# Head 0's mask adds spread over the attention units, with a new order of the attention and delta stages, in an fp32 hybrid encoder layer

## The chip, the cores and the metric

The program runs on one core of a Trainium2 chip as one launch. The metric is device time in microseconds (us). TensorE (PE) does matmuls, VectorE (DVE) and ScalarE (ACT) elementwise work, GpSimd (POOL) elementwise work in SBUF, and SyncE's queue (SP) issues all transfers. Each engine takes its instructions in the order written and waits on semaphores.

## The reference

One encoder layer on 1536 tokens (a prompt of 1024, a sample of 512), width 1024. The two stages that matter here are neighbourhood attention and the gated delta rule.

```python
def row_block(args):                      # attention: 8 heads of 64, windows of 8 x 16 positions
    s = jnp.einsum("bjqhd,bijkhd->bhjqik", q_r, k_r).astype(jnp.float32)
    s = jnp.where(col_ok[:, :, None, :], s + bias, -jnp.inf)
    p = jax.nn.softmax(s.reshape(s.shape[:4] + (kh * NA_KB,)), axis=-1).reshape(s.shape)
    return jnp.einsum("bhjqik,bijkhd->bjqhd", p.astype(v.dtype), v_r)
...
# delta rule: 4 heads of 128, both directions; g is the running sum of the log decay in a chunk
decay = jnp.exp(jnp.where(incl, g[..., :, None] - g[..., None, :], -jnp.inf))
a_mat = jnp.einsum("bhnid,bhnjd->bhnij", k_beta, k) * jnp.where(strict, decay, 0.0)
sol = lax.linalg.triangular_solve(eye + a_mat, rhs, left_side=True, lower=True, unit_diagonal=True)
qk = jnp.einsum("bhnid,bhnjd->bhnij", q, k) * decay
def step(s, xs):
    v_new = u_c - jnp.einsum("bhck,bhkv->bhcv", w_c, s)
    o = jnp.einsum("bhck,bhkv->bhcv", qd_c, s) + jnp.einsum("bhij,bhjv->bhiv", qk_c, v_new)
    s = s * jnp.exp(gl_c)[..., None] + jnp.einsum("bhck,bhcv->bhkv", kd_c, v_new)
```

Before them runs one large projection (`front`), after them the branch merge (`merge_project`) and the MLP (`mlp`). These three stay as they are.

## The kernel before

**Attention** (`attention`) works through 48 units: 4 pairs of heads, and in each pair 12 units (3 groups of rows by 4 blocks of columns). Unit `u` goes through the engines in a fixed pipeline: TensorE scores (line 1159), VectorE adds the bias table and takes the maximum (line 1216, signals `biased`), ScalarE exponentiates (1277), VectorE normalises (1230, `na_pn`), TensorE transposes (1201), ScalarE copies (1287), TensorE mixes with the values (1188), VectorE copies the result out (1254). In the first 8 units of a pair TensorE also transposes the values (1171) for VectorE to copy (1240). The bias tables lie in 4 buffers; a table is loaded (1089) when its buffer's last user has signalled `biased`. A unit whose table is missing stops VectorE. All loads stand in one written order on the sync queue.

Delta head 0 is prepared during attention. The rows of its log decay come by a broadcast load into `dn_gq` (line 1110, issued at unit 1). GpSimd adds two masks to 6 pieces of it, 12 instructions (`strict` and `incl`, line 1139), into `dn_kb`, as soon as the load has landed. At unit 6 VectorE makes the per-token columns of the decay (`decay_columns`, lines 999 to 1006, 8 chained instructions). From unit 8 ScalarE spreads 48 exponentials over the remaining units (1267).

**The delta stage** (`deltanet`) takes 4 heads in turn. A head has two parts. In the *solve* part, 18 positions `k` (three levels of 6 groups, in the order of `ORDER`) go through TensorE (1766), ScalarE (1651, 1654), TensorE (1782), VectorE (1968 or 1971), TensorE (1798) and ScalarE (1644): block inverses are joined to larger ones in `dn_un` and `dn_tn`. Tables give the position at which side work stands: `TURN_AT` where TensorE transposes keys and values (1731), `TOKEN_AT` where VectorE scales those (1939), `COLUMNS_AT` where VectorE makes the next head's columns, `EG_AT` where ScalarE exponentiates the decay rows (1667), and the tables of the output norm of the head before (`SQUARES_AT` to `GATE_AT`). The transposes of `TURN_AT` share one PSUM bank, so each waits until the one before has been scaled twice.

In the *chain* part, 8 steps run the recurrence: TensorE 1817, VectorE 1994, TensorE 1821, ScalarE 1680, TensorE 1828 to 1836, then VectorE 2006 (the state) and ScalarE 1687 (the output). Beside it the next head is prepared: Gram matrices (1744), scores and queries times the decays (VectorE 1884, 1894), the cut of small blocks into `dn_c` (1905, 1625), a widening transpose (1913), the small inverses on GpSimd (1541 to 1549, a chain of 30), two transposes back (1919, 1920), and the placing of the blocks in `dn_un` (VectorE 1932) and `dn_tn` (ScalarE 1635, GpSimd 1559). The solve part of the next head begins after the placing.

## Time and profile before

| | |
|---|---|
| median of 3 runs | 3051.58 us (3047.43 to 3055.48) |
| the profiled execution, its own time | 3052.57 us |
| its span, first to last instruction | 3050.9 us |
| TensorE busy | 2883.6 us, 95% |
| VectorE, ScalarE, GpSimd busy | 1299.3, 1072.3, 1204.7 us |
| attention, first score to last pair's end | 1094.5 to about 1240 us of the span |
| delta stage | 1240.5 to 1638.0 us of the span |

A page of the profile gives busy times by engine; a timeline gives the instructions of one engine in order of start, like neighbours merged (`x4`), with the idle time ahead of them in brackets and what ended it. The granted clock is TensorE's, as a share of 2.4 GHz.

### The profile page before, as it was taken

The page shows a single profiled execution, that of the slowest core. Times are in us where ns is not written, and L with a number is a line of the kernel's source. Part 1 is how long each engine was busy: PE and PEld are TensorE (multiplying, and loading weights), DVE is VectorE, ACT ScalarE, POOL GpSimd, SP SyncE. Part 2 cuts the span into 40 slices and gives each one's busy share as a digit, 9 for nine tenths or more (in the row PEclk, how much of TensorE's full clock was granted, in tenths as well). Part 3 has the DMA queues.
Part 4 walks back from the last instruction along what each step waited for, and adds up shares of the span by engine and source line. Part 5 has one row for each costly group of instructions (what it writes and reads, how often), then busy time and mean ns, then how long its engine had stood idle before and what let it go on. Part 6 is the DMA issues. An engine that isn't in the chain of part 4 may idle for free. (4 is left out here: it accounts for less than half of the span.)

```text
span 3050.9 us, 38569 instructions
## 1 busy us (share of the span) xinstructions
PE 2883.6 (95%) x15219; PEld 2351.4 (77%) x15219; DVE 1299.3 (43%) x1953; ACT 1072.3 (35%) x1829; POOL 1204.7 (39%) x805
## 2 busy tenths in 40 slices
PE   6999999999999969588778999999999999999998
PEld 5878787877888846477667887878888888888887
DVE  5233233221479959666664352322233232232323
ACT  4241313243044539455543122332332323233232
POOL 2222122121123320433422423466666676756663
PEclk9999999999999979778899999999999999999999
DMA  4434233343545357210113545332323333333331
GB/s 115 169 131 139 80 102 102 100 128 98 177 155 168 129 190 250 79 53 22 74 47 119 172 155 201 99 111 86 108 85 95 97 97 124 99 95 96 114 108 56
DMA packets 239572, 352.78 MB, mean 116 GB/s; under 512 B 32929, under 2 KB 186273, under 8 KB 239393
## 3 DMA queue, kind: packets, MB, share of 16 engines
q1 hardware_dynamic: 239392, 350.32, 35.3%
q8 instruction: 122, 2.00, 0.3%
q14 instruction: 58, 0.47, 0.0%
HBM read 263.71 MB, written 96.36 MB: 118 GB/s over the span
## 5 line engine op out<-in xcount | busy, mean ns | idle before, releaser
L102 PE MATMUL pj_acc<-u_hi,pj_w_hi 128*128 128x512 f32 x1464 | 576.4, 394 | 10.6 <-DVE u_lo L823 10.6
L2774 DVE TENSOR_TENSOR x_tm<-m_ps,x_tm 128x512 f32<-128x512 f32 x384 | 265.0, 691 | 744.2 <-PE m_ps L104 744.2
L104 PE MATMUL pj_acc<-u_hi,pj_w_lo 128*128 128x512 f32 x1464 | 571.8, 391 | 0.0
L103 PE MATMUL pj_acc<-u_lo,pj_w_hi 128*128 128x512 f32 x1464 | 571.2, 390 | 0.0
L551 POOL TENSOR_TENSOR pj_w_lo<-pj_w_raw,pj_w_hi 128x1024 fp32r<-128x1024 f32 x61 | 159.3, 2612 | 721.6 <-ACT pj_w_hi L600 721.6
L2656 POOL TENSOR_TENSOR m_lo<-gate,held 128x1024 fp32r<-128x1024 f32 x96 | 237.9, 2501 | 269.8 <-ACT held L2573 269.8
L102 PEld LDWEIGHTS pj_acc<-u_hi,pj_w_hi 128*128 128x128 f32 x1464 | 275.8, 188 | 85.6 <-issue 18.2
L104 PEld LDWEIGHTS pj_acc<-u_hi,pj_w_lo 128*128 128x128 f32 x1464 | 275.8, 188 | 58.2
L103 PEld LDWEIGHTS pj_acc<-u_lo,pj_w_hi 128*128 128x128 f32 x1464 | 276.1, 189 | 56.2
L102 PE MATMUL m_ps<-held 128*128 128x512 f32 x768 | 298.9, 389 | 2.4 <-DVEq L2755 2.4
L102 PE MATMUL m_ps<-held,m_h_hi 128*128 128x512 f32 x768 | 299.5, 390 | 0.0
L104 PE MATMUL m_ps<-held,m_h_lo 128*128 128x512 f32 x768 | 298.8, 389 | 0.0
L103 PE MATMUL m_ps<-m_lo,m_h_hi 128*128 128x512 f32 x768 | 298.8, 389 | 0.0
L104 PE MATMUL m_ps<-held,m_lo 128*128 128x512 f32 x768 | 298.8, 389 | 0.0
L103 PE MATMUL m_ps<-m_lo,held 128*128 128x512 f32 x768 | 298.8, 389 | 0.0
L2649 POOL TENSOR_TENSOR m_lo<-gate,held 128x1024 fp32r<-128x1024 f32 x92 | 218.5, 2396 | 0.0
L600 ACT CAST pj_w_hi<-pj_w_raw 128x1024 fp32r<-128x1024 f32 x61 | 63.9, 1047 | 374.6 <-PE pj_acc L104 374.6
L2573 ACT CAST held<-gate 128x1024 fp32r<-128x1024 f32 x96 | 96.1, 1050 | 253.7 <-PE m_ps L104 247.6
L2585 ACT CAST m_h_hi<-m_rel 128x512 fp32r<-128x512 f32 x96 | 59.6, 621 | 356.1 <-POOL m_rel L2662 356.1
L2317 POOL TENSOR_TENSOR mo_w_lo<-mo_w_raw,mo_w_hi 128x512 fp32r<-128x512 f32 x71 | 96.8, 1364 | 197.6 <-ACT mo_w_hi L2255 197.6
L102 PEld LDWEIGHTS m_ps<-held 128*128 128x128 f32 x768 | 144.1, 188 | 32.6 <-DVEq L2755 2.8
L103 PEld LDWEIGHTS m_ps<-m_lo,held 128*128 128x128 f32 x768 | 144.1, 188 | 30.1
(308 smaller groups left out, 4930.9 us busy)
## 6 DMA issues: line engine op xcount, KB each, us to landing
gate<-in_w_mlp_dram SPq DMA_DIRECT2D x48, 1024.0 KB, 5.4
gate<-in_w_mlp_dram SPq DMA_DIRECT2D x96, 512.0 KB, 3.7
proj<-pj_stage SPq DMA_DIRECT2D x61, 768.0 KB, 3.4
pj_w_raw<-in_w_in_dram SPq DMA_DIRECT2D x61, 512.0 KB, 5.2
gate<-proj SPq DMA_DIRECT2D x24, 768.0 KB, 4.4
mo_w_raw<-in_w_out_dram SPq DMA_DIRECT2D x48, 256.0 KB, 2.9
rpb_bias<-pj_shut SPq DMA_DIRECT2D x48, 192.0 KB, 3.0
rpb_bias<-rpb_near SPq DMA_DIRECT2D x24, 384.0 KB
```

Of the source, the lines that this page charges most:

```text
L102: pe.matmul(out, w_hi, x_hi, start=first, stop=False)
L103: pe.matmul(out, w_hi, x_lo, start=False, stop=False)
L104: return pe.matmul(out, w_lo, x_hi, start=False, stop=last)
L551: pool.tensor_tensor(w_lo[:, n % 2], w_raw[:, n % 2], w_hi[:, n % 2].bitcast(F32), ALU.subtract).then_inc(lo_done, 1)
L600: act.copy(w_hi[:, n % 2], w_raw[:, n % 2]).then_inc(hi_done, 1)
L2317: pool.tensor_tensor(w_lo[:, sl % 2], raw_w(sl), w_hi[:, sl % 2].bitcast(F32), ALU.subtract).then_inc(w_lo_done, 1)
L2573: act.copy(views.w2_hi(2 * gg + j), w2_raw[:, j].rearrange("p (a n) -> p a n", a=2)).then_inc(w2_hi_done, 1)
L2585: act.copy(h_hi[:, m % 4], rel[:, j]).then_inc(hh_done, 1)
L2649: pool.tensor_tensor(views.w1_lo(m), w1_raw[:, :, j * P:(j + 1) * P], views.w1_hi(m).bitcast(F32), ALU.subtract).then_inc(w1_lo_done, 1)
L2656: pool.tensor_tensor(views.w2_lo(m), w2_raw[:, j].rearrange("p (a n) -> p a n", a=2), views.w2_hi(m).bitcast(F32), ALU.subtract).then_inc( ...
L2774: dve.tensor_tensor(xt, ps2[:, q % 4], xt, ALU.add).then_inc(added, 1)
```

## The change

The log-decay columns are no longer copied for each head. Two tiles for all heads, `gneg` (minus g) and `gbeta` (g plus ln beta), are made at the start of attention by three VectorE instructions and one ScalarE logarithm; `cx`, also for all heads, is made once at the start of the delta stage, with two small matmuls that pick the chunk ends out. As ln beta is in the exponent, the scores are multiplied by one 128x512 instruction in place of four 128x128. In attention the loads of pair 1 move to units 4 and 6, the decay rows to unit 8, the exponentials to unit 14, and each mask add waits for a unit: the first for unit 9, each further one for two units more. In the delta stage the tables are new, the placing is split anew between VectorE and ScalarE, GpSimd's product with the queries (1531) is cut in three for each direction and starts after the placing, and the row exponentials move from the solve part to steps 5 and 6 of the chain before.

```diff
@@ attention
-    DG_AT, DCOL_AT, DY_AT, DEXP_AT = 1, 6, (28, 32, 36), 8
+    MASK_AT = 10
+    DG_AT, PAIR1_AT, DCOL_AT, DY_AT, DEXP_AT = 8, (4, 6), 6, (28, 32, 36), 14
...
-            for a in range(2):
-                load_qk(1, a)
-                load_v(1, a)
...
+                if u in PAIR1_AT:
+                    load_qk(1, PAIR1_AT.index(u))
+                    load_v(1, PAIR1_AT.index(u))
...
                 for q, mask in enumerate((strict, incl)):
+                    pool.wait_ge(biased, 2 * (MASK_AT + 2 * (2 * n + q)))
                     pool.tensor_tensor(dd0[:, 2 * n + q], gq[:, 0, d, tg * TB:(tg + 1) * TB].rearrange("p (j n) -> p j n", n=P),
...
+            dve.tensor_scalar(gbeta[:], cols[:, :, 2:4], 1e-30, None, ALU.max).then_inc(d_rates, 1)
+            dve.tensor_scalar(gneg[:], cols[:, :, 0:2], -1.0, None, ALU.mult).then_inc(d_cols, 1)
...
                 if u == DCOL_AT:
-                    dve.wait_ge(dg_in, 32)
-                    dc = Chain(dve, d_chain, 0, 8)
-                    decay_columns(dve, dc, cols[:, 0], col2[:, 0], ncol2[:, 0], cx2[:, 0], gq[:, 0])
-                    dve.sem_inc(d_cols, 1)
-                    dc.end()
+                    dve.wait_ge(d_rates, 2)
+                    dve.tensor_tensor(gbeta[:], cols[:, :, 0:2], gbeta[:], ALU.add).then_inc(d_cols, 1)
...
+            rates = gbeta[:].rearrange("p h d t -> p (h d t)")
+            act.wait_ge(d_rates, 1)
+            act.activation(rates, rates, ACT.Ln).then_inc(d_rates, 1)
@@ deltanet
-SQUARES_AT, ROOT_AT, EG_AT, CEXP_AT = 1, 5, (0, 2), 10
-LENGTHS_AT, MEAN_AT, DIAG_AT, SPREAD_AT, NORM_AT, GATE_AT = 2, 3, 5, (7, 9, 11), (8, 10, 12), 12
-TURN_AT = (0, 3, 6, 9, 11, 13)
-TOKEN_AT = ((1, 2), (4, 5), (7, 8), (10, 11), (12, 13), (14, 15))
-COLUMNS_AT = 6
-INCL_AT = {8: 4, 11: 5, 13: 0, 15: 1}
+SUM_AT, SQUARES_AT, LENGTHS_AT, MEAN_AT, ROOT_AT, DIAG_AT = 0, 2, (3, 4, 5), 6, 8, 8
+SPREAD_AT, NORM_AT, GATE_AT = (10, 12, 14), (11, 13, 15), 15
+TURN_AT = (0, 2, 5, 8, 11, 13)
+TOKEN_AT = ((0, 1), (2, 3), (5, 6), (9, 10), (11, 12), (13, 14))
+INCL_AT = {9: 4, 12: 5, 15: 0}
...
-INCL_END = {1: 3, 3: 2}
+INCL_END = {1: 1, 3: 3, 4: 2}
...
-QK_IN = {0: (4, 5), 1: (0, 1), 4: (3, 2)}
+QK_IN = {0: (4, 5), 2: (0, 1), 5: (3, 2)}
...
+EG_IN = (5, 6)
...
+                for q in Q32:
+                    act.copy(by_direction(un, q, 0)[:, 0:NTB:2, :, q], compact(c1, q, 0)[:, 0:NTB:2]).then_inc(S["un0_d0"], 1)
+                act.wait_ge(S["spread"], 2 * i + 2)
                 for q in Q32:
                     act.copy(by_direction(tn, q, 0)[:, :, :, q], compact(c2, q, 0)).then_inc(S["tn0_act"], 1)
...
-                for j in range(4):
-                    last = dve.scalar_tensor_tensor(am[:, n, j], ps[:, 4 + 2 * (GRAMS.index(tg) % 2), j],
-                                                    ncol2[:, i % 2, 2 + d, 4 * tg + j:4 * tg + j + 1], decays[:, j], ALU.mult, ALU.mult)
-                last.then_inc(S["am_done"], 1)
+                dve.scalar_tensor_tensor(am[:, n], ps[:, 4 + 2 * (GRAMS.index(tg) % 2)], -1.0, decays, ALU.mult,
+                                         ALU.mult).then_inc(S["am_done"], 1)
...
-                if i:
-                    out_sum(i - 1)
...
+                        if k == SUM_AT:
+                            out_sum(i - 1)
```

The sync engine's queue in the first attention pair, before: the rows behind the first bias tables (`na_bias`) are pair 1's queries, keys and values, then the decay rows.

```order
L1089 DMA na_bias<-rpb_bias 128x2x384
L1075 DMA na_qt<-proj 128x512
L1075 DMA na_kt<-proj 128x768
L1080 DMA na_vt<-proj 128x2x384
L1080 DMA na_vt<-v_mid 128x2x384
L1075 DMA na_qt<-proj 128x1024
L1075 DMA na_kt<-proj 128x768
L1080 DMA na_vt<-proj 128x2x384
L1080 DMA na_vt<-v_mid 128x2x384
L1110 DMA dn_gq<-g_rows 128x1536 x2
L1089 DMA na_bias<-rpb_bias 128x2x384 x2
L1089 DMA na_bias<-rpb_bias 128x2x256 x3
```

The same place of the queue after the change.

```order
L1077 DMA na_bias<-rpb_bias 128x2x384 x3
L1077 DMA na_bias<-rpb_bias 128x2x256
L1063 DMA na_qt<-proj 128x512
L1063 DMA na_kt<-proj 128x768
L1068 DMA na_vt<-proj 128x2x384
L1068 DMA na_vt<-v_mid 128x2x384
L1077 DMA na_bias<-rpb_bias 128x2x256
L1063 DMA na_qt<-proj 128x1024
L1063 DMA na_kt<-proj 128x768
L1068 DMA na_vt<-proj 128x2x384
L1068 DMA na_vt<-v_mid 128x2x384
L1077 DMA na_bias<-rpb_bias 128x2x256
```

Four bias loads now stand ahead of the first of pair 1's loads, and one more between the two halves; before, one did, and the next came behind the decay rows.

VectorE in the solve part of delta head 0, from the last two positions of level 0, before.

```order
L1968 COPY_PREDICATED dn_un<-join,dn_ps 128x512
L1939 TENSOR_TENSOR dn_kb<-dn_ps,dn_col 128x512
L1971 COPY dn_un<-dn_ps 32x4x32 x2
L999 COPY dn_col<-cols 128x48
L1000 TENSOR_SCALAR dn_ncol<-dn_col 128x48
L1004 COPY dn_cx<-dn_col 128x12
L1005 TENSOR_TENSOR dn_cx<-dn_gq,dn_col 128x12
L1006 COPY dn_cx<-dn_gq 128x12
L1004 COPY dn_cx<-dn_col 128x12
L1005 TENSOR_TENSOR dn_cx<-dn_gq,dn_col 128x12
L1006 COPY dn_cx<-dn_gq 128x12
L1971 COPY dn_un<-dn_ps 32x4x32 x2
```

The same place after the change.

```order
L1971 COPY_PREDICATED dn_un<-join,dn_ps 128x512
L1950 TENSOR_TENSOR dn_kb<-dn_ps,cols 128x512
L1971 COPY_PREDICATED dn_un<-join,dn_ps 128x512 x2
L1950 TENSOR_TENSOR dn_kb<-dn_ps,dn_cx 128x512
L1974 COPY dn_un<-dn_ps 32x4x32 x2
L1950 TENSOR_TENSOR dn_kb<-dn_ps,dn_cx 128x512
L1974 COPY dn_un<-dn_ps 32x4x32 x6
L1950 TENSOR_TENSOR dn_kb<-dn_ps,cols 128x512
```

The eight column instructions between two positions of level 1 are gone, and the scalings `dn_kb` stand closer behind the positions.

ScalarE in steps 2 to 7 of the chain beside which the next head is prepared, after the change (`dn_nb` and `oz` are the recurrence's own copies).

```order
L1668 COPY dn_nb<-dn_ps 128x128 x4
L1617 COPY dn_c<-dn_am 32x384 x4
L1677 COPY oz<-dn_ps 128x128 x4
L1668 COPY dn_nb<-dn_ps 128x128 x4
L1677 COPY oz<-dn_ps 128x128 x4
L1591 ACTIVATE dn_qk<-dn_qk,dn_gneg 128x128 x4
L1668 COPY dn_nb<-dn_ps 128x128 x2
L1677 COPY oz<-dn_ps 128x128 x2
L1591 ACTIVATE dn_qk<-dn_qk,dn_gneg 128x128 x4
...
L1606 ACTIVATE dn_gq<-dn_gq 128x1536
L1668 COPY dn_nb<-dn_ps 128x128 x2
L1677 COPY oz<-dn_ps 128x128 x2
L1606 ACTIVATE dn_gq<-dn_gq 128x1536
```

The cut (`dn_c`) stands ahead of step 2's output copies where it stood behind them, and the two row exponentials (`dn_gq`) stand in steps 5 and 6, where there were none.

## Rows read from the trace of the kernel before

**Rows 1.** The page of the whole execution: its span, and the granted clock in 40 slices.

```profile
span 3050.9 us, 38569 instructions
...
PEclk9999999999999979778899999999999999999999
```

**Rows 2.** Windows: length, busy us of PE, PEld, DVE, ACT, POOL, clock, DMA.

```profile
1094.50:1145.00 50.50, 35.27 (x232) 22.11 (x232) 33.19 (x100) 21.66 (x66) 16.36 (x17) 0.75 0.63 223
1145.00:1174.90 29.90, 29.90 (x266) 19.74 (x266) 27.05 (x105) 26.97 (x88) 0.00 (x0) 1.00 0.75 238
...
1240.50:1276.10 35.60, 7.49 (x48) 7.14 (x48) 20.18 (x44) 3.54 (x7) 19.50 (x38) 0.63 0.36 141
1276.10:1321.65 45.55, 38.77 (x569) 33.80 (x569) 24.43 (x57) 25.96 (x69) 21.81 (x14) 0.69 0.01 2
1321.65:1359.40 37.75, 32.80 (x250) 29.68 (x248) 28.38 (x77) 20.01 (x72) 11.75 (x30) 1.00 0.00 1
...
1364.50:1419.50 55.00, 44.91 (x598) 37.02 (x599) 29.44 (x65) 29.82 (x72) 23.23 (x14) 0.75 0.20 76
...
1462.90:1515.20 52.30, 42.68 (x599) 35.86 (x600) 29.31 (x65) 29.70 (x72) 23.22 (x14) 0.79 0.21 79
...
1558.20:1603.70 45.50, 37.64 (x583) 30.88 (x583) 27.96 (x56) 20.21 (x43) 8.28 (x2) 0.84 0.20 69
```

**Rows 3.** Timeline, VectorE, first attention pair: start, us, instruction, idle before.

```profile
1119.56 0.56 DVE L1216 CUSTOM_DVE_ANT_0 na_sc<-na_ps_s,na_bias 128x384 f32<-128x384 f32 x1 [7.91 <-DMA na_bias<-rpb_bias]
...
1120.71 1.78 DVE L1230 TENSOR_SCALAR na_pn<-na_pr,na_rinv 128x384 f32<-128x384 f32 x2
...
1124.22 2.19 DVE L1230 TENSOR_SCALAR na_pn<-na_pr,na_rinv 128x384 f32<-128x384 f32 x2
...
1127.72 1.09 DVE L999 COPY dn_col<-cols 128x48 f32<-128x48 f32 x1
...
1133.76 0.16 DVE L1006 COPY dn_cx<-dn_gq 128x12 f32<-128x12 f32 x1
...
1135.51 0.75 DVE L1230 TENSOR_SCALAR na_pn<-na_pr,na_rinv 128x384 f32<-128x384 f32 x2
```

**Rows 4.** Timeline, the sync engine's queue, first attention pair.

```profile
1104.40 1.45 SPq L1110 DMA_DIRECT2D dn_gq<-g_rows  x2
1105.90 18.60 SPq L1089 DMA_DIRECT2D na_bias<-rpb_bias  x5
```

**Rows 5.** Timeline, GpSimd, first and last of head 0's twelve mask adds.

```profile
1118.45 1.26 POOL L1139 TENSOR_TENSOR dn_kb<-dn_gq,strict 128x512 f32<-128x512 f32 x1 [22.52 <-DMA dn_gq<-g_rows]
...
1132.39 1.26 POOL L1139 TENSOR_TENSOR dn_kb<-dn_gq,incl 128x512 f32<-128x512 f32 x1
```

**Rows 6.** Timeline, VectorE, one normalising multiply beside a mask add.

```profile
1121.08 1.42 DVE L1230 TENSOR_SCALAR na_pn<-na_pr,na_rinv 128x384 f32<-128x384 f32 x1
```

**Rows 7.** Waits of TensorE in the delta stage: total us, times, longest.

```profile
PE dn_ps L1766 <- DVE dn_un L1932: 40.8, 4, 25.6
PE dn_ps L1731 <- DVE dn_kb L1939: 21.6, 13, 3.9
```

**Rows 8.** Timeline, VectorE, delta stage, heads 0 and 1.

```profile
1290.37 0.99 DVE L999 COPY dn_col<-cols 128x48 f32<-128x48 f32 x1
...
1294.44 0.59 DVE L1971 COPY dn_un<-dn_ps 32x128 f32<-32x128 f32 x2 [0.26 <-DVE dn_cx L1006]
...
1334.75 2.15 DVE L1884 SCALAR_TENSOR_TENSOR dn_am<-dn_ps,dn_ncol,dn_am 128x128 f32<-128x128 f32 x8
...
1362.74 4.86 DVE L1932 COPY dn_un<-dn_c 32x256 f32<-32x256 f32 x16
```

**Rows 9.** Timeline, ScalarE, delta stage, head 0's row exponential.

```profile
1277.90 1.48 ACT L1667 ACTIVATE dn_gq<-dn_gq 128x1536 f32<-128x1536 f32 x1
```

**Rows 10.** Timeline, VectorE, the output gate of two heads.

```profile
1406.54 2.30 DVE L1869 SCALAR_TENSOR_TENSOR oz<-oz 128x1536 f32<-128x1536 f32 x1
...
1594.11 1.76 DVE L1869 SCALAR_TENSOR_TENSOR oz<-oz 128x1536 f32<-128x1536 f32 x1
```

More of the change, by code:

```diff
@@ L1682, in main @@
                         strict_decays(i + 1, STRICT_MID[step])
+                    if more and step == CUT_IN:
+                        cut_blocks(i + 1)
                     for j, d, t in live_chains(step):
@@ L1701, in _ @@
             act.wait_ge(mixed_landed, 16)
-            act.sem_inc(S["cexp"], 1)
             act.sem_inc(S["exp_s"], NG6)
             act.sem_inc(S["exp_i"], NG6)
+            act.wait_ge(S["columns"], 5)
+            flat_cx = cx[:].rearrange("p h a t -> p (h a t)")
+            act.activation(flat_cx, flat_cx, ACT.Exp).then_inc(S["cexp"], 1)
+            for d in range(2):
+                row_decays(0, d)
             cut_blocks(0)
@@ L1836, in main @@
                         pe.matmul(o, nb[:, j], qk2[:, i % 2, 2 * (t // 4) + d, t % 4], start=step == 0, stop=True).then_inc(S["o_mm"], 1)
+            pe.wait_ge(S["ends"], 2)
+            for d in range(2):
+                last = pe.matmul(ps[:, 3, d, 0:HEADS * NT], work[:, d * P:(d + 1) * P], cols[:, :, d], start=True, stop=True)
+            last.then_inc(S["ends"], 1)
             for x in range(NTB):
@@ L1984, in main @@
                             out_gate(i - 1)
-                    if k == COLUMNS_AT and more:
-                        columns(i + 1, nxt)
                 dve.sem_inc(S["s0"], 1)
@@ L2039 @@
                 K_KEPT.append((_step, _j))
-K_DN = 1 + 7 + 1
 class MlpViews:
```

173 lines of the change are left out of this document (84 added, 89 removed).

## The prediction

> **What bounds the kernel now.** I read the page first. The span is 3050.9 us, and the clock row has its dip in the slices of the delta stage [rows 1]. TensorE is busy 95% of the span, so only time in which it waits, or runs at a lower clock, can be won. The windows say where: the first attention pair's disturbed stretch takes 50.50 us at a granted clock of 0.75, and the next equal piece of work 29.90 at 1.00, PE busy throughout. The stretch in which delta head 0 is prepared takes 35.6 us with PE busy for 7.49. The four solve parts take 45.55, 55.00, 52.30 and 45.50 us at clocks of 0.69 to 0.84, head 0's chain part 37.75 us with 32.80 of PE [rows 2].
>
> Then the waits. In the attention stretch VectorE stands still for 7.91 us at 1119.56 for a bias table, and 8 column instructions fill it from 1127.72 to 1133.92 [rows 3]. In the delta stage TensorE waits 40.8 us in 4 waits for the placing of blocks (the longest, 25.6, is head 0's) and 21.6 us in 13 waits for the scalings of keys and values [rows 7].
>
> **The change part by part.** The sum is made against the profiled execution, 3052.57 us, 1.0 above the median.
>
> *Attention, loads.* The first bias table that VectorE waits for stands behind pair 1's loads and the decay rows; the five bias issues occupy the queue from 1105.90 for 18.60 us [rows 4]. Now four tables stand ahead of pair 1. The wait of 7.91 should go: −7.9. What is late next: pair 1's own queries and keys, wanted only about 20 us after the last of them is issued, and the decay rows, issued after unit 8 for a first mask at unit 9 and exponentials at unit 14. At 29.9/12 = 2.5 us a unit the last have some 12 us to land; if late, ScalarE, which works in order, would hold the probabilities back. I count nothing.
>
> *Attention, columns.* Seven of the eight chained instructions go from VectorE, 1127.72 to 1133.92 [rows 3]; −6.2. One addition of 128x96 stays; its nearest rows are 0.16 us (128x12) and 1.09 (128x48, beside GpSimd), and I take +0.5 for it and the three at the start. ScalarE's logarithm and the return to its exponential stand before the first score's exponential, where nothing is ready: 0.
>
> *Attention, masks.* Before, the twelve adds run from 1118.45 to 1133.65 [rows 5], partly inside the bias wait. Normalising multiplies beside them take 1.78 and 2.19 us the pair, 0.75 later without them [rows 3]: 1.78 + 2.19 − 1.50 = 2.5 us. In one go that is −2.5 when they leave. The whole gain of loads, columns and contention is 7.9 + 6.2 − 0.5 + 2.5 = 16.1, and with an estimated 1 for the clock of 0.75 in that stretch 17; its bounds are 14 (the wait and the columns alone) and 20.6 (50.50 − 29.90 [rows 2]).
>
> Spread, each add is released by `biased` of the last head of a unit, just as VectorE ends that addition and turns to the normalising multiply. So the add of 1.26 us falls on a multiply nearly every time, and a single multiply beside an add takes 1.42 in place of 0.75/2 = 0.38 [rows 6]: 1.04 us, twelve times 12.5. VectorE is busy 27.05 of 29.90 us in a steady stretch, 0.24 us a unit to spare, and TensorE has no idle time at all in it [rows 2]. The delay can therefore be hidden only in part, in the buffers between engines. Bounds: 0 (all in buffers) and 12 × 2 × 1.04 = 25 (both multiplies of a unit hit). I take 10, between 12.5 and that slack (12 × 0.24 = 2.9). Attention: −17 + 10 = −7.
>
> A rule speaks against this part too. The Trainium skill, "SBUF — State Buffer", section "SBUF: two separate sides", says that VectorE and GpSimd share a port pair, and that some of VectorE's fast or two-input instructions and a GpSimd instruction lock it against each other for the whole instruction. By that rule the multiply waits for the add's end, 1.26 + 0.38 = 1.64 at worst; the trace's 1.42 is close to it. By it the twelve would cost 15 in place of 12.5.
>
> *Head 0's preparation.* 35.6 us before [rows 2]. The 8 multiplies of 128x128 become 2, the row exponentials come before the cut, and two tiny matmuls for the chunk ends, with VectorE's copies for them, stand ahead of the Gram matrices. With the multiply's eight at 2.15 us [rows 8] as a gain of about 1, and one exponential of 1.48 [rows 9] plus about 1 for the ends as a loss: +1, bounds −2 to +4.
>
> *Placing.* VectorE's 16 copies take 4.86 us (0.30 each) [rows 8] and end what TensorE waits for. Less head 0's 25.6, the other three waits sum to 15.2, 5.1 a head [rows 7]. Now ScalarE places one part of `dn_un` after the first narrowing transpose while VectorE does the other after the second; the copies are about halved on each path. I take a third of the 4.86, 1.6 a head, four times −6; bounds 0 and −10 (half of it, 2.4, each).
>
> *Columns in the solve part.* Head 0's set for head 1 runs from 1290.37 until the next position's copy at 1294.44, 0.26 us of idle time among it [rows 8]; the position it holds back is on the path: about 3 of the 4.07 us, since some of it fits the loop's slack. In heads 1 and 2 no GpSimd work lies beside it and each is nearer 1: −5, bounds −2 and −10.
>
> *Turns and scalings.* The 21.6 us in 13 waits [rows 7] come where `TURN_AT` and `TOKEN_AT` leave a transpose waiting for a scaling of the position just before it, or the same. In the new tables turns and scalings stand one to three positions apart except at 11 and 13, where the columns are also gone. I take −13 of the 21.6, bounds −5 and −20.
>
> *Row exponentials.* In the solve part's opening ScalarE works on one of 1.48 us [rows 9] before positions' squares, −2 in all for a part of 1.48 in some heads. In the chain they now stand in steps 5 and 6, where ScalarE is busy 20.01 of 37.75 us [rows 2]: two of 1.48 are cheap unless an output copy or `dn_nb` waits behind one. The cut goes ahead of step 2's copies, am falls from 2.15 for 8 to perhaps 1.4 (its four reads are the same bytes, three starts are saved). Net +1 for the chain parts, bounds −3 and +9 (3 heads × 2 × 1.48).
>
> *Out_sum behind position 0 and the tables of the norm.* These are VectorE instructions that take the columns' place in the early positions. Where GpSimd works beside VectorE a large one lasts longer: 2.30 against 1.76 [rows 10]. A third-size piece has 0.2 to 1 us extra; it is in the bounds, not in the sum. The page just named, in the same section, would make such pieces wait for all of a GpSimd product; no row of before shows that pairing.
>
> *Clock.* Solve parts run at 0.69 to 0.84, that is partly at 1.2 GHz, and chains at 1.00 [rows 2]. Each low stretch follows a wait in which TensorE stood. Fewer waits, shorter low stretches: PE is busy 38.77 of 45.55 us at 0.69 in head 0. I take −5 for all; bounds 0 and −20, as head 3's part at 0.84 needs 37.64 of PE where heads 1 and 2 need 44.91 and 42.68 with head-norm work included.
>
> Sum: −7 + 1 − 6 − 5 − 13 − 2 + 1 − 5 = −36. 3052.57 − 36 = 3016.6 for a profiled execution, 3016 for the median.
>
> **The rivals.**
> *A, the clock stays up* (0.10). If the removed waits are those after which the clock falls, the solve parts would come near the PE time of full clock: for it speaks that the dips in [rows 1] lie only in this stage; against, that other waits (the solve loop's own, head 0's 25.6) remain. It would give 20 in place of 5 and some of the attention bounds: 2998 or less.
> *B, the small gain* (0.13). Each mask add hits both multiplies (25 in place of 10, net +8), and the row exponentials hold up steps 5 and 6 (+9 in place of +1). Then −36 + 15 + 8 = −13: 3039. For it: a pair of multiplies among back-to-back adds went from 0.75 to 2.19 [rows 3], 1.44 more and so more than one hit. Against: an add of 1.26 us is over when the multiply of 1.42 that it meets is, and the buffers between engines take some.
> *C, it doesn't do what it says* (0.08). The solve loop runs from engine to engine at its own latency; with the scaling waits gone, TensorE waits for the next position instead. Head 3's part, which has no next head's turns, still takes 45.50 [rows 2]. Then turns and columns give 4 in place of 18 (+14), the clock nothing (+5), placing half (+3), the opening nothing (+2) and head 0's preparation costs its upper bound (+3): −36 + 27 = −9, 3043, no change that can be told.
> *D, slower* (0.07). One mechanism: the chain parts fall to 1.2 GHz. Now they start from a solve part whose side work is elsewhere, and exponentials and cuts in ScalarE's order stop TensorE in steps 2, 5 and 6. A chain holds 32.80 us of PE at clock 1.00 [rows 2]; at 1.2 GHz that work is nearly twice as long, less the 5 us of idle time that it fills: 32.8 − 5 = about +28 each. One chain would give 3044, two 3072. The 36 us won are outweighed from 1.3 chains on, so it takes two. Against it: before, chains keep 1.00 in spite of the waits in them.
>
> **How the numbers follow.** Main forecast 3016, its own range 3000 to 3032, from the sum's bounds taken together, not all at their ends: 0.62. Between the cases: A 0.10 below 3000, B 0.13, C 0.08, D 0.07. The range 2994 to 3037 leaves out part of A, C, D and half of B. A measurement of this kernel tells about 0.3% from no change: 3042.4 to 3060.7. Main, A and B lie below it: 0.85; C lies within: 0.08; D is above: 0.07.
>
> **What would show each step right or wrong.** Attention: no wait of VectorE for a bias table above 1 us, no columns, and a first pair of about 33 us for the stretch that took 50.5; multiplies of 1.4 us beside the twelve adds, one a second unit. Delta: the placing waits after head 0's at 3.5 or less; the scalings' waits under 9 in all; solve parts of about 41, 48, 47 and 43; chain parts within 1 of before, clock 1.00. The prediction is wrong if masks cost nothing or twice as much in the pairs' lengths, if the waits for scalings come back under another name (for squares, or for `dn_un`), if the decay rows land late, or if the clock of the chains falls below 1.

## The result and the profile after

| | before | after |
|---|---|---|
| median | 3051.58 us | 3034.57 us |
| four runs | 3047.43 to 3055.48 | 3030.89 to 3036.73 |
| ratio | | 0.9942, 95% interval 0.9926 to 0.9958 |
| span of the profiled execution | 3050.9 us | 3031.9 us |

The change wins 17 us, 0.6%. The forecast was 3016 (-36), with a range of 2994 to 3037. The sign is right and the range holds the time, but the main case's own range, 3000 to 3032, does not, and the gain is less than half of what was worked out.

The page of the changed kernel, its span and granted clock [rows 1]:

```profile
span 3031.9 us, 38463 instructions
...
PEclk9999999999999999798879999999999999999999
```

The windows of the changed kernel, one for each stage: attention, head 0's preparation, then solve part and chain part of each head in turn (a chain part here reaches to the next solve part, so it holds the placing), and last all that follows. Columns as in [rows 2].

```profile
1093.70:1228.75 135.05, 124.79 (x1056) 80.28 (x1056) 118.75 (x416) 106.43 (x336) 16.39 (x18) 0.97 0.68 232
1228.75:1267.96 39.21, 9.32 (x54) 9.01 (x53) 19.82 (x30) 6.79 (x12) 19.06 (x38) 0.62 0.33 128
1267.96:1301.95 33.99, 32.15 (x568) 28.00 (x569) 21.09 (x48) 23.16 (x64) 22.96 (x19) 0.85 0.01 2
1301.95:1342.83 40.88, 33.64 (x250) 30.29 (x249) 29.17 (x61) 25.73 (x84) 13.33 (x34) 0.99 0.03 12
1342.83:1391.94 49.11, 41.05 (x599) 34.33 (x599) 29.45 (x56) 23.75 (x57) 24.35 (x19) 0.83 0.25 95
...
1433.47:1485.63 52.16, 43.67 (x598) 35.77 (x599) 29.48 (x56) 23.88 (x57) 24.35 (x19) 0.76 0.24 90
...
1527.02:1579.66 52.64, 44.88 (x582) 36.89 (x583) 29.71 (x56) 19.18 (x43) 9.38 (x7) 0.71 0.10 33
1579.66:1619.79 40.13, 31.51 (x217) 28.42 (x217) 15.74 (x43) 17.28 (x56) 1.27 (x1) 0.92 0.25 85
1619.79:3031.90 1412.11, 1396.96 (x6174) 1153.94 (x6174) 446.83 (x535) 414.71 (x568) 811.83 (x475) 0.99 0.35 113
```

The same stages of both kernels, lengths in us, cut at the same instructions in the windows of either trace:

| stage | before | after | difference |
|---|---|---|---|
| attention | 144.99 | 135.05 | -9.9 |
| head 0's preparation | 36.58 | 39.21 | +2.6 |
| solve part 0 | 45.51 | 33.99 | -11.5 |
| solve part 1 | 55.09 | 49.11 | -6.0 |
| solve part 2 | 52.24 | 52.16 | -0.1 |
| solve part 3 | 45.44 | 52.64 | +7.2 |
| chain parts 0 to 2 | 129.25 | 123.80 | -5.5 |
| chain part 3 | 38.60 | 40.13 | +1.5 |
| merge and MLP (same code) | 1408.63 | 1412.11 | +3.5 |

The reader is to see that TensorE's instructions are the same in both solve parts 3 (some 583 matmuls), yet its busy time rose from 37.64 [rows 2] to 44.88 us and the clock fell from 0.84 to 0.71; its idle time in that part stayed at 7.8 us. The gain shrinks from solve part to solve part, and the last one is slower than before. The merge and MLP differ by 3.5 us with the same code. In the other traces below this stretch is either 1408.6 to 1410.7 or 1411.8 to 1412.9, in kernels that differ only far ahead of it. TensorE is busy for 1396.96 us of the 1412.11 here, and for 1393.87 of 1409.03 with the same instructions in one of the kernels below, so the difference is in its clock. One profiled execution carries some 3 us of such chance, and what follows goes by medians and by single stages.

The waits of TensorE in the changed kernel, which answer to [rows 7]:

```profile
PE dn_ps L1762 <- ACT dn_un L1628: 31.0, 4, 23.4
...
PE dn_ps L1725 <- DVE dn_kb L1950: 7.1, 4, 2.9
...
PE dn_ps L1762 <- ACT dn_ss L1650: 5.4, 4, 2.5
PE dn_ps L1738 <- DVE dn_un L1974: 5.2, 3, 2.5
```

The waits for scalings fell from 21.6 to 7.1 us, as forecast. But what is left of them is one wait a head, 0.5, 1.4, 2.3 and 2.9 us, at position 2. The waits for the last copy of the solution grew, to 2.5 us in heads 1 and 2 and 3.1 in head 3, 8.3 in all where the kernel before had 2.0.

What makes the wait at position 2 is seen on VectorE. Timeline, VectorE, start of solve part 3 of the changed kernel:

```profile
1532.59 0.68 DVE L1950 TENSOR_TENSOR dn_kb<-dn_ps,dn_cx 128x512 f32<-128x512 f32 x1
1533.18 2.85 DVE L1848 TENSOR_TENSOR oz<-oz 128x1536 f32<-128x1536 f32 x1
1535.95 0.72 DVE L1971 COPY_PREDICATED dn_un<-join,dn_ps 128x512 f32<-128x512 uint8 x1
1536.58 0.67 DVE L1950 TENSOR_TENSOR dn_kb<-dn_ps,dn_cx 128x512 f32<-128x512 f32 x1
```

The output's sum (line 1848), which the change put behind position 0, takes 2.85 us. Position 1's copy and the second scaling stand behind it, and TensorE's turn at position 2 wants that scaling. Timeline, TensorE, same place:

```profile
1537.30 0.66 PE L1725 MATMUL dn_ps<-ident,dn_yn 128*128 128x128 f32 x4 [2.89 <-DVE dn_kb L1950]
```

And what follows. Windows of the changed kernel from that wait to the end of solve part 3:

```profile
1537.30:1540.00 2.70, 2.70 (x40) 2.44 (x40) 1.29 (x2) 2.30 (x5) 2.33 (x2) 0.74 0.03 6
1540.00:1564.00 24.00, 24.00 (x280) 19.74 (x279) 10.45 (x21) 8.59 (x22) 0.00 (x0) 0.50 0.01 2
1564.00:1579.66 15.66, 11.81 (x133) 9.05 (x132) 9.44 (x16) 3.30 (x9) 0.00 (x0) 0.94 0.04 14
```

For 24 us TensorE is busy without a gap, at half of full clock, 1.2 GHz (27.3 us with the ends of the stretch, from 1538.59 on). This is where the missing gain was looked for.

### The profile page after: what moved, and what is told of

Same layout as the page of the kernel before. It is cut to its first block and busy times, and to the rows that moved or that the text cites. A ratio compares the mean times of both kernels' runs of the same rounds, so it can differ in the third digit from the quotient of the medians.

```text
span 3031.9 us, 38463 instructions
## 1 busy us (share of the span) xinstructions
PE 2885.8 (95%) x15223; PEld 2351.7 (78%) x15223; DVE 1286.8 (42%) x1840; ACT 1079.6 (36%) x1845; POOL 1205.9 (40%) x821
## 5 line engine op out<-in xcount | busy, mean ns | idle before, releaser
L104 PEld LDWEIGHTS m_ps<-held,m_lo 128*128 128x128 f32 x768 | 144.6, 188 | 30.1
```

The lines of the kernel that those rows point to most:

```text
L104: return pe.matmul(out, w_lo, x_hi, start=False, stop=last)
```

## The experiments

The theory after reading the trace: the sum behind position 0 is what eats the gain, by a wait and by the low clock that goes with it. The rivals: the spread mask adds eat it in attention; the clock falls in this stage whatever the order; the new positions of turns and scalings won nothing. Each kernel was timed in 5 rounds beside the kernel before, whose medians were 3051.1, 3051.3, 3052.1, 3052.4 and 3051.6 in the five sets. Unless said otherwise an edit is made to the changed kernel alone.

### Mask adds in one go

```diff
             pool.wait_ge(dg_in, 32)
+            pool.wait_ge(biased, 2 * MASK_AT)
             for n in range(2 * NTB):
...
-                    pool.wait_ge(biased, 2 * (MASK_AT + 2 * (2 * n + q)))
```

> The changed kernel, with head 0's twelve mask adds in one go from unit 10 on instead of one for every second unit. Theory (spread adds cost): in the changed kernel the lead of 18.6 us at the 52nd score matmul shrinks to 10 at the end of attention, which I put down to the twelve multiplies stretched beside adds. In one go about 6 multiplies are hit, as before: attention 135.0 to about 129 us, the whole 6 us faster than the changed kernel, 3028. Rival (the adds are free, the lead is lost to something else, such as late keys or exponentials that start at unit 14): attention stays within 2 us of 135, the time at 3034.

Measured: 3025.94 us, ratio 0.9918 (0.9903 to 0.9932), 9 us faster than the changed kernel. Attention took 132.01 us against 135.05. Windows, attention of this kernel:

```profile
1094.73:1226.74 132.01, 127.14 (x1056) 82.43 (x1056) 114.44 (x416) 106.35 (x336) 16.60 (x18) 0.94 0.69 237
```

So the spreading does cost, but 3 us in its own stage, half of what was expected; 3.5 of the other microseconds in the profile lie in merge and MLP. This is spread against in one go, and not against no adds at all: in one go they still meet 8 multiplies and stretch them by 6.5 us in all, spread they meet 11 and stretch them by 11.7. VectorE's busy time fell by 4.3 us, from 118.75 to 114.44.

How an add is paid for is seen in the changed kernel's trace. Timeline, GpSimd, one spread add:

```profile
1150.50 1.27 POOL L1128 TENSOR_TENSOR dn_kb<-dn_gq,incl 128x512 f32<-128x512 f32 x1 [5.10 <-DVE na_nmax L1207]
```

Timeline, VectorE, the multiplies of the unit before, with no add beside them, and of the unit with it:

```profile
1147.67 0.75 DVE L1221 TENSOR_SCALAR na_pn<-na_pr,na_rinv 128x384 f32<-128x384 f32 x2
...
1150.53 1.78 DVE L1221 TENSOR_SCALAR na_pn<-na_pr,na_rinv 128x384 f32<-128x384 f32 x2
```

1.78 against 0.75: 1.03 us a hit, as forecast (1.04), and the add starts 0.03 us ahead of the multiplies, with 1.24 us left to run when they start.

### The sum ahead of position 0

```diff
             def main(i, more):
+                if i:
+                    out_sum(i - 1)
                 for k in range(NS):
...
-                        if k == SUM_AT:
-                            out_sum(i - 1)
```

> The changed kernel, with the sum of the output (VectorE, 128x1536) ahead of position 0 of the solve part, where it was before the change, instead of behind position 0. Theory (a new wait, and the clock after it): TensorE's waits for a scaling at position 2 (1.4, 2.3 and 2.9 us in heads 1, 2 and 3) go, and with the last of them head 3's stretch of 24 us at 1.2 GHz gets shorter: 6 us for the waits and 6 to 10 for the clock, 3034 to about 3021. Rival (the clock falls in this stage whatever the waits, so only waits count, and the sum delays the first positions instead): the waits go but 2 us a head come at position 0, no change within 3 us.

Measured: 3013.24 us, ratio 0.9891 (0.9872 to 0.9911), 21 us faster by the medians. The five runs lie at 3011.69 to 3013.24 and at 3023.17 and 3024.86, all below the changed kernel's lowest, 3030.89. This is the largest effect of all. The waits for scalings went from 7.1 to 1.8 us. Timeline, VectorE, start of its solve part 3:

```profile
1521.57 1.76 DVE L1848 TENSOR_TENSOR oz<-oz 128x1536 f32<-128x1536 f32 x1
1523.24 0.73 DVE L1973 COPY_PREDICATED dn_un<-join,dn_ps 128x512 f32<-128x512 uint8 x1
```

And its windows, solve parts 1, 2 and 3:

```profile
1341.16:1386.96 45.80, 38.22 (x598) 31.60 (x599) 28.61 (x56) 23.84 (x57) 24.36 (x19) 0.89 0.28 102
1429.43:1475.40 45.97, 38.23 (x599) 31.61 (x599) 28.61 (x56) 23.70 (x57) 24.35 (x19) 0.89 0.27 101
1518.01:1558.07 40.06, 34.69 (x582) 28.75 (x583) 28.59 (x56) 18.94 (x43) 9.38 (x7) 0.91 0.13 45
```

Against the changed kernel's 49.11, 52.16 and 52.64 us they are 22.1 us shorter. TensorE's busy time makes up 18.5 of that (129.6 to 111.1), idle time only 3.6. It is not the chance of one trace: solve parts 1 to 3 take 153.9, 147.1 and 153.9 us in the changed kernel and in the two below that differ from it in attention alone, and 131.8 and 131.9 in the two with the sum ahead and the other tables as they are. So the rival is wrong in that the clock does depend on the order, and the theory had the clock's part too small: it is five times the waits'.

### The gate behind the last position

```diff
-SPREAD_AT, NORM_AT, GATE_AT = (10, 12, 14), (11, 13, 15), 15
+SPREAD_AT, NORM_AT, GATE_AT = (10, 12, 14), (11, 13, 15), 17
```

> The changed kernel, with the output gate behind the last position (17) instead of behind position 15, where it holds back the last two copies of the solution. Theory: the waits of 2.49, 2.49 and 3.05 us at the end of the solve parts 1 to 3 go, about 7 us, and some 3 for the clock at the start of the chains: 3034 to 3025. Rival (the gate of 1.76 us only moves into the chain's first step and is waited for there): within 2 us of the changed kernel.

Measured: 3035.94 us, ratio 0.995 (0.9936 to 0.9963): no change, as the rival said. The waits for the last copy fell from 8.3 to 2.9 us, and came back in the chain's first step. Waits of TensorE there, head 1:

```profile
PE dn_ps L1824 <- ACT dn_nb L1668: 3.4, 1, 3.4
```

In the changed kernel this wait is 0.9. The chain parts of heads 1 to 3 grew by 3.7 to 4.1 us each. In its trace solve part 3 took 39.29 us against 52.64, though the wait at position 2 was there, 2.25 us: the long stretch at 1.2 GHz did not follow it this time.

### Old positions of turns and scalings

```diff
-TURN_AT = (0, 2, 5, 8, 11, 13)
-TOKEN_AT = ((0, 1), (2, 3), (5, 6), (9, 10), (11, 12), (13, 14))
+TURN_AT = (0, 3, 6, 9, 11, 13)
+TOKEN_AT = ((1, 2), (4, 5), (7, 8), (10, 11), (12, 13), (14, 15))
```

> The changed kernel with the positions of turns and scalings of the kernel before. Theory (the new positions removed most of the 21.6 us of waits): the waits for scalings rise from 7.1 to about 16 us (the eight column instructions that made the largest ones are gone in any case), and the kernel is 8 to 12 us slower than the changed one, 3043. Rival (these waits only stood in for others, the loop is bound by its latency): within 3 us of 3034.

Measured: 3047.44 us, ratio 0.999 (0.9981 to 1.0), 13 us slower than the changed kernel. The waits for scalings rose to 12.8 us. The new positions are worth 13 us, and nearly all of the change's net gain hangs on them. The trace is of the slowest of eleven runs, and here too the clock is part of the price: in solve part 2 it shows 47.8 us at 0.50, with TensorE busy for 42.1 of them.

### Both edits at once

> Both edits at once: the mask adds in one go and the output's sum ahead of position 0. Alone they gave medians of 3025.94 and 3013.24 against the changed kernel's 3034.57, -9 and -21, of which 3 to 4 in each profile lie after the delta stage in code that is the same. Theory (two separate costs that add): 3013 minus the 3 us that attention gained alone, and up to 9: 3005 to 3010. Rival (part of each gain was a luckier clock, which can be won only once): 3011 to 3016.

Measured: 3009.56 us, ratio 0.9874 (0.9859 to 0.9888). On top of the sum's edit the adds in one go are worth 3.7 us, which fits attention's 131.65 against 135.64. By this reckoning some 5 of the 9 us of the first experiment were the clock's chance.

### The norm's steps earlier

On top of both edits:

```diff
-SUM_AT, SQUARES_AT, LENGTHS_AT, MEAN_AT, ROOT_AT, DIAG_AT = 0, 2, (3, 4, 5), 6, 8, 8
-SPREAD_AT, NORM_AT, GATE_AT = (10, 12, 14), (11, 13, 15), 15
+SUM_AT, SQUARES_AT, LENGTHS_AT, MEAN_AT, ROOT_AT, DIAG_AT = 0, 1, (2, 3, 4), 4, 6, 6
+SPREAD_AT, NORM_AT, GATE_AT = (8, 10, 12), (9, 11, 13), 13
```

> The kernel with both edits, and the output norm's steps 1 or 2 positions earlier, so that the gate stands behind position 13 instead of 15. Theory: the wait of 2.5 us (3.05 in head 3) for the last copy of the solution in each of the solve parts 1 to 3 shrinks by the gate's 1.76 us, and the stretch of 4 us at 1.2 GHz behind it goes: 3 heads x (1.8 + 2) = 11 us faster than the kernel with both edits. Rival (with the gate behind the last position nothing was won, since the wait and the low clock only came 1 step later; here they come at position 14): within 3 us.

Measured: 2999.07 us (2998.41 to 3000.07), ratio 0.9828 (0.9815 to 0.9841): 10.5 us faster than with both edits, 35.5 faster than the changed kernel. Against the kernel with only the sum's edit, TensorE's waits for the last copy fell from 8.3 to 1.2 us and those for ScalarE's copies around the root (line 1650) from 5.5 to 0.4, while the waits of line 1778 for the copies of the other positions rose from 0.8 to 7.2. So half of the waiting moved and half went. Against the kernel with both edits the solve parts are only 1.2 us shorter in all; most of the gain is in the chain parts behind heads 1 to 3 (1.6 to 2.0 us each) and in merge and MLP, 3.5 us of the clock's chance in this one trace.

### GpSimd's product later

```diff
                 pool.wait_ge(S["un0_late"], 4 * i + 4)
+                pool.wait_ge(S["u_ev"], i * NS + 3)
                 decayed_queries(i)
```

> The changed kernel, in which GpSimd's product with the queries starts three positions later, so that the sum behind position 0 runs alone. Theory A (the sum costs by the contention with GpSimd: it takes 2.5 to 2.85 us against 1.76 alone, and the wait of 1.4 to 2.9 us for the scaling of position 2 is made by this): the sum takes 1.76, the wait falls to 0.7 to 1.8, and the long stretch at 1.2 GHz in head 3 shortens: 8 to 15 us faster than the changed kernel, 3022. Theory B (the place alone counts): the sum's 1.76 us still hold back position 1's copy and the second scaling, the waits stay above 1 us and the time within 4 us of 3034.

Measured: 3021.78 us, ratio 0.9902 (0.9889 to 0.9915), 13 us faster. Timeline, VectorE, the sum in solve part 3:

```profile
1534.87 1.75 DVE L1849 TENSOR_TENSOR oz<-oz 128x1536 f32<-128x1536 f32 x1
```

It stands in the same place as in the changed kernel, and takes 1.75 in place of 2.85 us, with no GpSimd work beside it. So some 13 of the 21 us that the sum's place costs go when the product is not under way. In the trace all of it lies in part 3 (39.97 us against 52.64); part 1 is 2.2 us longer. That the place itself makes the other 8 is not shown: the four runs, 3021.61 to 3021.87, lie between the upper and the lower runs of the kernel with the sum ahead, and the intervals overlap.

What counts is which of the two starts first. Timeline, VectorE and GpSimd, solve part 1 of the kernel before:

```profile
1367.63 1.76 DVE L1848 TENSOR_TENSOR oz<-oz 128x1536 f32<-128x1536 f32 x1
1367.86 4.85 POOL L1531 TENSOR_TENSOR dn_gq<-dn_gq,dn_yn 128x1536 f32<-128x1536 f32 x1 [4.62 <-issue]
```

The sum starts 0.23 us ahead of the product and keeps its 1.76 us; the product takes 4.85 where it takes 3.43 by itself. So it is with the sum ahead of position 0 in the new tables: the product starts 0.10 us behind it, and the sum takes 1.76. Behind position 0 the sum comes second, and it is the sum that waits.

### Pair 1's loads first

```diff
             load_bias(3)
+            for a in range(2):
+                load_qk(1, a)
+                load_v(1, a)
             for u in range(U + 4):
...
-                if u in PAIR1_AT:
-                    load_qk(1, PAIR1_AT.index(u))
-                    load_v(1, PAIR1_AT.index(u))
```

> The changed kernel with pair 1's loads back ahead of the waiting table loads; the decay rows stay at unit 8. Theory (the wait for the bias table comes from pair 1's 4.5 MB in the queue): a wait of 5 to 8 us of VectorE for a table comes back in the first pair, and the lead of attention falls from 10 to 3 us: 3041. Rival (the decay rows were what stood in its way, or the columns were most of the gain): attention stays at 135, 3034.

Measured: 3034.12 us (3024.23 to 3040.89), ratio 0.994 (0.9926 to 0.9953). The median says no change; the stage says otherwise. Timeline, VectorE, first pair of this kernel:

```profile
1095.51 0.56 DVE L1207 CUSTOM_DVE_ANT_0 na_sc<-na_ps_s,na_bias 128x384 f32<-128x384 f32 x1 [5.24 <-DMA na_bias<-rpb_bias]
1114.18 0.56 DVE L1207 CUSTOM_DVE_ANT_0 na_sc<-na_ps_s,na_bias 128x384 f32<-128x384 f32 x1 [3.65 <-DMA na_bias<-rpb_bias]
```

The first wait is there in the changed kernel too (5.3 us, for the first scores). The second is the old one, smaller. Attention took 141.85 us, 6.8 more. (Pair 1's loads come to 3.1 MB by their shapes, not to the 4.5 of the expectation.) In that execution, the slowest of the six, the whole span was 3039.2, 7.3 more than the changed kernel's; over six runs, which lie 17 us apart, this is not seen. The 6.8 us are shown for the stage and not for the whole.

### Columns back

On top of the sum's edit, a chain of eight instructions behind position 6 (the last line also shows the call):

```diff
+            def again(i):
+                c = Chain(dve, S["again"], i, 8)
+                c.link(dve.tensor_copy(again_a[:], cols[:, i + 1]))
+                c.add(dve.tensor_scalar(again_b[:], again_a[:], -1.0, None, ALU.mult))
+                for d in range(2):
+                    c.add(dve.tensor_copy(again_c[:, d], again_a[:, d]))
...
+                    if k == 6 and more:
+                        again(i)
```

> The kernel with the sum ahead of position 0, and behind position 6 of the first three solve parts a chain of eight small VectorE instructions of the shapes and count of the old column instructions, which write to tiles of their own that nobody reads (they are work on top, for the size of the columns' term). Theory (a term of its own, as predicted 5 us): the chain takes about 2.5 us where no GpSimd work lies beside it and up to 4 where it does, a wait for position 6 or for a scaling comes of it in each head, 5 us and some clock: 3013 to 3020. Rival (the loop has slack at that place): within 3 us of 3013.

Measured: 3020.69 us, ratio 0.9901 (0.9886 to 0.9915), 7.5 us slower than the 3013.24; in the traces the delta stage differs by 3.5 us. The runs of the two kernels overlap, 3015.64 to 3022.9 here and 3011.69 to 3024.86 there, so the 7.5 is not clear of noise. The forecast's 5 for this term lies between the two figures and is not contradicted.

### Early norm and late product

> The best kernel so far (2999.07: adds in one go, sum ahead, norm early), with GpSimd's product three positions later. Theory (contention was paid by the large sum alone; with the sum ahead of position 0 the product meets only copies of under 1 us): within 3 us of 2999. Rival (the product slows the copies and scalings of the first positions too): 3 to 8 us faster, 2993.

Measured: 2997.66 us (2996.84 to 3010.46), ratio 0.9837 (0.9816 to 0.9857): by the medians the same as without the late product. But the runs fall apart, three at 2996.84 to 2997.66 and two at 3007.53 and 3010.46, where the four of the kernel without it lie within 1.7 us. The trace is of one of these two. Timeline, VectorE and GpSimd, its solve part 1:

```profile
1356.97 6.34 DVE L1859 TENSOR_TENSOR dn_work<-ident,dn_ors 128x1536 f32<-128x1536 f32 x1
1354.27 7.43 POOL L1510 TENSOR_TENSOR dn_qk<-dn_gq,incl 128x512 f32<-128x512 f32 x6
```

An instruction that takes 1.76 us by itself came up in the middle of six GpSimd instructions and took 6.34, until 1.6 us after the last of them. Solve part 1 took 55.42 us against 44.93, with 20.5 us at 1.2 GHz. So the late product takes the contention from the sum and can put it on the next large instruction.

### The sum's move alone, in the kernel before

```diff
             def main(i, more, c, nxt):
-                if i:
-                    out_sum(i - 1)
                 for k in range(NS):
...
                     if i:
+                        if k == 0:
+                            out_sum(i - 1)
                         if k == MEAN_AT:
```

> The kernel before, with only the output's sum moved from ahead of position 0 to behind it. In it the first scaling stands at position 1 and GpSimd's products start as soon as the row exponentials of positions 0 and 2 are there. Theory (the sum at position 0 costs when a scaling is wanted at position 2 and the product runs beside it; here the next turn is at position 3): 0 to 4 us slower, 3053. Rival (holding back position 1's copy costs in any order of turns): 6 to 20 us slower, 3062.

Measured: 3074.67 us, ratio 1.0081 (1.0067 to 1.0095): 23 us slower than the kernel before. The theory, that the old turns would shield it, is wrong: the waits for scalings stayed (20.3 us against 21.6). Timeline, VectorE, start of its solve part 1:

```profile
1367.72 3.64 DVE L1848 TENSOR_TENSOR oz<-oz 128x1536 f32<-128x1536 f32 x1
1371.29 0.72 DVE L1966 COPY_PREDICATED dn_un<-join,dn_ps 128x512 f32<-128x512 uint8 x1
```

The product of 3.43 us started first, at 1366.31, and had 2.02 us left when the sum started; the sum takes 3.64. ScalarE's squares of that sum stand at position 1, and the loop's own copies queue behind them: TensorE's waits for those (line 1651) grew from 2.4 us to 13.4. Solve parts 1 to 3 are 21.2 us longer in all, 11.4 of it TensorE's busy time. So the move costs about the same 21 to 23 us in both kernels, by one wait or by another.

### The sum behind position 0 in the last head alone

```diff
-                        if k == SUM_AT:
+                        if k == SUM_AT and i == HEADS - 1:
                             out_sum(i - 1)
```

with the sum ahead of position 0 in heads 1 and 2.

> The kernel of 3013.24 (the sum ahead of position 0), with the sum behind position 0 in the last head alone, as the changed kernel has it in three. Theory (a wait of 2.9 us at position 2 is followed by a long stretch at 1.2 GHz, so it costs far more than itself; that part took 52.64 us against 40.06): 8 to 13 us slower than 3013, 3023. Rival (the long low stretch of that one trace was chance, and a wait costs itself): 1 to 4 us slower, 3016.

Measured: 3024.39 us, ratio 0.9921 (0.9907 to 0.9936): 11 us slower for one instruction moved by one position in one head. All stages ahead of the last solve part agree with those of the 3013.24 within 0.3 us; that part took 52.25 us against 40.06, the chain part behind it 41.55 against 39.92. Windows, from the wait on:

```profile
1529.55:1533.30 3.75, 3.75 (x62) 3.35 (x64) 2.60 (x4) 2.37 (x6) 2.34 (x2) 1.00 0.02 4
1533.30:1561.30 28.00, 28.00 (x322) 22.05 (x317) 12.08 (x25) 9.90 (x26) 0.00 (x0) 0.53 0.01 1
```

Where the clock falls, in windows of 2 us:

```profile
1533.00:1535.00 2.00, 2.00 (x42) 1.76 (x41) 0.84 (x2) 0.99 (x3) 0.00 (x0) 0.98 0.00 0
1535.00:1537.00 2.00, 2.00 (x28) 1.61 (x28) 0.07 (x1) 0.72 (x2) 0.00 (x0) 0.50 0.00 0
```

The cost is as the theory said, and its reason for it is not: here the wait for the scaling was only 1.06 us, TensorE then ran 5.4 us at full clock without a gap, and the clock fell all the same, for some 27 us.

### The one-column matmuls

The two long low stretches shown above have one thing in common: in them lie the output's lengths, 24 matmuls with one column each, 8 at each of positions 3, 4 and 5. Two kernels put all of them at position 3, or at 6 with the mean at 7:

```diff
-                        if i and k in LENGTHS_AT:
-                            out_lengths(i - 1, LENGTHS_AT.index(k))
+                        if i and k == 3:
+                            for tb in range(NTB):
+                                out_lengths(i - 1, tb)
```

> The changed kernel, with all 24 one-column matmuls of the output's lengths at position 3, where it has 8 each at positions 3, 4 and 5. Theory T (they lie in every long low stretch of the changed kernel, and spread over three positions they keep TensorE's clock low once a late scaling has made it wait): head 3's stretch of 24 us at 1.2 GHz is gone, 8 to 12 us faster than 3034.57. Theory W (the waits alone decide, whatever lies behind them): within 3 us of it.

> The changed kernel, with all 24 one-column matmuls at position 6 and the mean one position later, farther from the late scaling at position 2. Theory T (thin matmuls right behind the wait keep the clock low): 8 to 15 us faster than 3034.57. Theory W (the waits alone): within 3 us of it, with the low stretch of head 3 in its place behind position 2.

Measured: 3031.44 us, ratio 0.9936 (0.9924 to 0.9949), and 3029.76 us, ratio 0.9936 (0.9923 to 0.995). Both intervals overlap the changed kernel's. In the traces solve part 3 got shorter (47.19 and 43.82 against 52.64) and with the lengths at position 3 part 1 got longer (58.04 against 49.11). The traces are of the slowest of five runs and of the fastest of six. In neither is a stretch of 24 us at 1.2 GHz left: the longest in solve parts 1 to 3 are 13.7 us and 10.2 us, though the waits at position 2 are up to 2.8 and 2.6 us. The medians are 3.1 and 4.8 us below the changed kernel's, where theory T wanted 8 at least and theory W at most 3. Neither theory is shown. Against the matmuls as the whole cause speaks solve part 0 of the kernel before, which has none of them:

```profile
1297.60:1321.49 23.89, 20.81 (x172) 18.16 (x171) 7.96 (x18) 11.96 (x39) 7.57 (x6) 0.50 0.01 1
```

## Why the prediction was off, step by step

**The step that failed** is the one named "Out_sum behind position 0 and the tables of the norm". It gave a piece "0.2 to 1 us extra", and put it "in the bounds, not in the sum". Moving the sum costs 21 us (taken back, 3034.57 to 3013.24) or 23 (done alone to the kernel before). Three things were missed. The piece is not "a third-size piece" but the whole sum, 128x1536, stretched from 1.76 us to 2.51, 2.54 and 2.85. It was costed by how much longer the instruction gets, not by who stands behind it: in the changed kernel the second scaling, which TensorE wants at position 2, and with the old tables ScalarE's squares and the copies behind them. (That the new `TURN_AT` wants the scaling one position earlier is not the reason, since the move costs as much with the old one.) And of the cost 18.5 of 22.1 us are not waiting but working at 1.2 GHz. That "no row of before shows that pairing" holds for the rows and not for the trace: there the product starts 0.23 us behind the sum and gives way to it.

With the sum's place taken back the kernel stands at 3013.24, 3 us from the forecast of 3016. That is partly luck: the solve parts are then 34.4 us shorter than before, where columns, turns, row exponentials and clock together were put at 25, and 22.9 of the 34.4 are in TensorE's busy time, for which the clock's term had 5. Merge and MLP gave back 3.4 in that trace. Head 0's solve part, which has no sum, was forecast at about 41 us and took 34.0.

**Attention, net -7**: measured -9.9. The size of a hit was right, 1.03 us, and so was that nearly each add meets a multiply (11 of 12, 11.7 us in all). The split into -17 and +10 was against a kernel without any adds, which was not run. Measured is spread against in one go: attention takes 131.62 to 132.28 us in the four kernels in one go, a mean of 131.9, and 135.05 to 136.69 in nine with the adds spread, a mean of 135.8. The 3.9 us between them come with 4.3 us more of VectorE's busy time, so hardly anything of the delay was hidden in the buffers between the engines. In one go 6.5 to 6.8 us of stretching remain, where the kernel before had 2.6. If those cost at the same rate as the rest, an estimate from these figures, the spread adds cost some 9 us and loads and columns won some 19, both near the forecast. The bound of 20.6 for the latter was less firm than it looked: the two stretches of "equal" work hold 232 and 266 matmuls [rows 2].

How long a hit lasts follows what is left of the GpSimd instruction: 1.24 us left and 1.03 more for the multiplies, 2.02 left and 1.89 more for the sum of 3.64. The Trainium skill, "SBUF — State Buffer", section "SBUF: two separate sides", says that of a GpSimd instruction and a VectorE one with two SBUF inputs or in a two-port mode, whichever starts first has the shared ports for its whole length and the other waits. The traces agree in both directions, and in the 6.34 us of the late product four such instructions in a row came first.

**Head 0's preparation, +1**: +2.6, inside its bounds.

**Placing, -6**: right. The three waits after head 0's fell from 15.1 to 7.6 us in all, with 2.3 more behind the first matmuls, so -5.2 without head 0; head 0's fell by 2.2.

**Turns and scalings, -13**: right in size, and undoing the positions alone costs 13. The waits fell by 14.5 us, but 6.3 of it came back as waits for the last copy of the solution, behind the output gate that now stands at position 15. The prediction had named that, waits under another name for `dn_un`, as a sign of being wrong.

**Columns, -5**: not contradicted, 3.5 in the traces and 7.5 in medians that overlap.

**Row exponentials, -2, and the chain parts, +1**: without the waits for the placing the first three chain parts are 0.6 to 0.8 us longer each, 2.0 in all. Neither was tried alone.

**Clock, -5**: wrong in both directions. In the changed kernel TensorE's busy time in the four solve parts is 161.8 us against 164.0 before, so 2; with the sum ahead it is 141.1, so 23. Rival A, in which the solve parts come near the time of full clock, is nearer to what the kernel with the sum ahead does than its 0.10 suggests. Its reason, that the clock follows the waits that were removed, is not shown.

**Rivals**: B came nearest to the time (3039), for reasons that did not hold: the spread adds did not hit both multiplies of a unit, and steps 5 and 6 at most a part of 2.0 us. C is refuted by the old positions' 13 us. D did not happen: chain parts 0 to 2 kept 0.98 to 0.99.

**What stays open**: why the clock stays low for 20 to 48 us, and in which head. In head 3 a stretch of 27.3 us followed a wait of 2.89 us in one trace and, 5.4 us later, one of 1.06 in another; a wait of 2.25 at the same place (the gate last) was followed by full clock. With the adds in one go, and the delta stage as in the changed kernel, the long stretch stood in head 1 and not in head 3. In the kernel with the late product a wait of 1.65 in head 3 was followed by full clock, and one of 0.62 in head 1 by 20 us at half. The length of the single wait does not decide it, nor do the one-column matmuls alone. Shown is that the sum's place changes how much of the solve parts runs at 1.2 GHz, and not by what way.

## What to carry to other kernels

Cost a moved instruction by what is queued behind it on its engine and which engine wants that next, not by how much longer it takes itself, and look for the next one in the queue of the engine that reads its result too. Put a large VectorE instruction where the engine it feeds is at work on something long, here ahead of position 0, and so that it starts ahead of the long GpSimd work and not behind it; when you move the GpSimd work instead, look which large instruction it meets next. When a stage runs partly at 1.2 GHz, a wait's price is not its length: read TensorE's busy time of equal work in both traces, since it shows what the clock took. And before you say what a delay costs, look whether the kernel you compare with has it in part: the adds in one go still stretched VectorE's work by 6.5 us.

## What was unexpected of the hardware

A stretch of 24.00 us with TensorE busy for 24.00 at a granted clock of 0.50, and one of 28.00 us at 0.53, in which the clock fell 5.4 us after the last wait. One instruction of 1.76 us, moved by one position in one head, made 11 us of difference in the median. The same sum took 1.76 us when it started 0.10 or 0.23 us ahead of GpSimd's product and 3.64 when it started 1.41 us behind; another instruction of 1.76 us took 6.34 in the middle of six GpSimd instructions. The merge and the MLP, the same code in all kernels, took either 1408.6 to 1410.7 or 1411.8 to 1412.9 us.
